# One expert slot fewer per layer, with the experts ordered by the row counts of three tiles

## The chip, the cores and the metric

The kernel runs on one core of one Trainium2 chip. The metric is the time of one execution in microseconds on the device. TensorE multiplies, VectorE, ScalarE and GpSimd do the element work, and the 16 DMA engines of the core move data. GpSimd issues the indexed transfers (gathers and scatters), ScalarE the stores and loads of whole row blocks, and SyncE the loads of weights.

## What is computed

The reference is one step of a two-layer decoder for a prompt group of 512 rows and a sample group of 64 rows, with the same weights for both and all arithmetic in float32. A layer has a mixer (spatial gating and differential attention) and then a mixture of 16 experts, which is where the change is:

```python
h = rmsnorm(x, g2).reshape(b * t, d)
pg = jax.nn.softmax((h @ r_g), axis=-1)          # 4 groups: the best one is taken
le_sel = ...                                     # the 4 experts of that group
tw, ti = lax.top_k(jax.nn.softmax(le_sel), 2)    # the best two of them
eidx = gi[:, None] * E_PER + ti
hg = jnp.einsum('nd,edf->nef', h, w_gate)
hu = jnp.einsum('nd,edf->nef', h, w_up)
a = jax.nn.silu(hg) * hu * gates[..., None]
return jnp.einsum('nef,efd->nd', a, w_down)
```

Each of the 576 rows goes to two experts of one group. An expert's weights are 1024 x 512 (gate and up) and 256 x 1024 (down).

## The kernel before

The 576 rows lie in five tiles of 128 (tile 4 holds the 64 sample rows). The order in which the tiles leave the mixer is `SEQ`: 0, 1, 2, 4, 3. For each tile TensorE multiplies by the output weights (`out_rows`, `sample_out`), VectorE adds (`add_out`), TensorE turns the tile (`turn_rows`) and computes router logits (`logit_parts`, `logit_sums`, `logits`), and VectorE marks the two experts of each row (`chosen`, result `M`). `token_ranks` sums `M` on TensorE, which gives every row its place among its expert's rows. ScalarE stores the normalised rows of each tile to `h_rows` (`store_rows`); the last store counts in `h_last`.

The experts are worked off in slots of 128 row places (`SLOTS`; an entry is a list of position, first row and width). A slot is one expert of up to 128 rows, or two or three parts of experts that share the 128 places. Positions are filled with experts by their row counts (`by_size` writes `order`); positions 0, 1 and 2 are fixed to the experts 0, 1 and 2 (`STILL`). There are 14 slots. Per slot: VectorE compares places with a row of numbers (`hot`, `main_group`), TensorE turns that into row indices (`index_rows`), VectorE writes them (`index`), GpSimd gathers the slot's rows (`gather_main`), TensorE turns them (`turn_in`), VectorE scales (`in_turned`), TensorE multiplies by gate and up in two halves (`up`), ScalarE and VectorE gate, TensorE turns (`turn_act`) and multiplies by down (`down`), ScalarE evacuates (`result`) and GpSimd scatters to `y_rows`. In a shared slot the parts are written as matmuls of 32 or 64 columns beside each other. The loop of TensorE runs `up` of slot n, `turn_act` of slot n-1, `up` second half, `index_rows` at slots 1, 3 and 5, `turn_in` of slot n+1, `down` of slot n-1.

The first slot is gathered earlier: `first_index` gives the rows of tiles 0, 1, 2 and 4, `gather_first` fetches them while the last tile is still in the mixer, `first_turn` turns them, and `first_late` adds the rows of the last tile.

SyncE loads the weights in pieces of 1 MB, three for each expert, in the order of first use (`LOADS`) into ten buffers. It waits at three places: for the end of the attention before the first piece, for `h_last` before the seventh, and for `order` before the first piece whose address depends on it. In the sample attention `sample_combine` writes the tile `fold`, which TensorE needs for `sample_turn`. `keep_busy` issues matmuls whose result nobody reads.

Of the kernel before, what the change touches and what calls it, by code (L numbers as in the profile page):

```python
# [19 lines left out]
P = 128  # L20
# [43 lines left out]
for _n, _w in _PAR:  # L64
# [5 lines left out]
NC32 = 8 * P + 64 + NT * 4 + 32 + E * E + 3 * E + 20  # L70
# [5 lines left out]
C_TIE, C_BASE, C_CAP = (slice(C_CLASS.stop + i * E, C_CLASS.stop + (i + 1) * E) for i in range(3))  # L76
C_PARTS = slice(NC32 - 20, NC32)
# [3 lines left out]
STILL = 3  # L81
CLASSES = [[0], [1], [2], [e for e in range(STILL, E) if e % EG != EG - 1], [e for e in range(E) if e % EG == EG - 1]]
FIRST_PLACE = [0, 1, 2, STILL, E - G]
SLOTS = [[(0, 0, 128)], [(1, 0, 128)], [(2, 0, 128)], [(3, 0, 128)], [(7, 0, 96), (3, P, 32)], [(4, 0, 128)], [(9, 0, 64), (10, 0, 64)], [(5, 0, 128)],
         [(6, 0, 128)], [(11, 0, 64), (15, 0, 64)], [(8, 0, 96), (12, P, 32)], [(12, 0, 128)], [(13, 0, 128)], [(14, 0, 128)]]
# [119 lines left out]
def program(nc, totals, d):  # L205
    Count.loops, Count.every, Count.layer = [], [], 0
    with ExitStack() as ctx:
# [70 lines left out]
        order_of = cat_cols[:, 256:512].rearrange("p (n e) -> p n e", n=E)  # L278
        moved = cat_cols[:, 3840:3840 + NT * (E - STILL) * E].rearrange("p (t n e) -> p t n e", t=NT, n=E - STILL)
# [108 lines left out]
        STEADY, EXTRA_BUFFERS = (6, 5, 7, 4, 8, 9, 2, 0, 3, 1), (2, 3, 6, 7, 8, 9)  # L388
        AHEAD = [4, 0, 5, 1, 2, 3]
# [53 lines left out]
        def _(sp):  # L443
# [8 lines left out]
            for l in layers():  # L452
                expert_at = {}
                for i in [*(AHEAD if l else range(RING)), *range(RING, W_LAYER)]:
# [24 lines left out]
                    if i >= N_DENSE:  # L479
                        pos, part = LOADS[i - N_DENSE]  # L480
                        if pos >= STILL:
                            if pos not in expert_at:
                                if not expert_at:
                                    sp.wait_ge(*dve_s.at("order"))
                                expert_at[pos] = sp.value_load(order[0:1, pos:pos + 1], min_val=0, max_val=E - 1)
                            at = expert_at[pos] * PER_EXPERT + (l * W_LAYER + N_DENSE + part)
                        else:
                            at = l * W_LAYER + N_DENSE + pos * PER_EXPERT + part
# [214 lines left out]
        def _(pe):  # L703
# [44 lines left out]
            for l in layers():  # L748
# [309 lines left out]

                def first_index():
# [36 lines left out]
                def after_sample(k):  # L1096
# [3 lines left out]
                    if k == HALF + 1:  # L1100
                        logit_sums(1)

                def after_last(n, k):
                    if (n, k) == (0, 2):
# [1182 lines left out]
```

## Time and profile before

| | us |
|---|---|
| median of 3 runs | 987.95 (983.75 to 988.01) |
| profiled execution | 987.82 |
| its span | 986.0 |
| PE busy | 946.2 (96%) |
| DVE busy | 397.1 (40%) |
| ACT busy | 249.4 (25%) |
| POOL busy | 191.9 (19%) |

PE is TensorE's matmul side, DVE VectorE, ACT ScalarE, POOL GpSimd, SPq SyncE's own queue. Times in a timeline are microseconds from the start of the span. The two layers repeat each other: what stands at time t in layer 0 stands about 485 us later in layer 1.

### The profile page before, as it was taken

How to read it: one execution, taken by the hardware profiler on the slowest of the kernel's cores; microseconds unless marked ns; L12 is line 12 of the kernel's file. 1: busy time of each engine (PE TensorE's matmuls, PEld its weight loads, DVE VectorE, ACT ScalarE, POOL GpSimd, SP SyncE). 2: the span in 40 equal slices, each digit the busy share in tenths (PEclk: the TensorE clock that was granted, in tenths of full speed). 3: DMA queues.
4: the chain of work that ended last, by engine and by line, in shares of the span. 5: the costliest groups of instructions: out<-in, count | busy, mean ns of one | idle time of the engine just before them, and what ended most of it. 6: DMA issues, size and time to landing. Idle time of an engine off the chain costs nothing.

```text
span 986.0 us, 12965 instructions
## 1 busy us (share of the span) xinstructions
PE 946.2 (96%) x4672; PEld 469.9 (48%) x4672; DVE 397.1 (40%) x991; ACT 249.4 (25%) x499; POOL 191.9 (19%) x267
## 2 busy tenths in 40 slices
PE   9999999999999999999899999999999999999991
PEld 6444445556445444434554344455564454444340
DVE  2403235676446562111343122556663575511114
ACT  2112346542011111111121123656221012111110
POOL 2333201331101111111124032023220012111100
PEclk9999999999999999999999999999999999999996
DMA  9716003341613979997842150225243169799946
GB/s 346 271 35 266 1 1 134 100 159 51 270 44 147 361 266 367 419 420 321 277 155 74 40 228 0 91 87 172 56 177 132 65 258 339 279 383 415 410 166 236
DMA packets 39769, 197.53 MB, mean 200 GB/s; under 512 B 7652, under 2 KB 7780, under 8 KB 23824
## 3 DMA queue, kind: packets, MB, share of 16 engines
q1 hardware_dynamic: 19456, 136.02, 35.2%
q0 software_dynamic: 15888, 45.80, 13.3%
q10 hardware_dynamic: 4352, 14.76, 4.2%
q8 instruction: 42, 0.69, 0.3%
q14 instruction: 31, 0.25, 0.1%
HBM read 177.24 MB, written 29.88 MB: 210 GB/s over the span
## 4 chain that ended last, share of the span: by engine, by line
PE 88%; DVE 5%; issue 2%; DMA 2%; ACT 1%; POOL 0%; POOLq 0%; DVEq 0%; ACTq 0%
PE ps L710 79%; PE ps L708 7%; PE ps L726 2%; DMA cat<-y_rows 1%; DVE cat L1933 1%; DMA hT<-h_rows,igat 1%; DVE hT L2075 0%; DMA y_rows<-hn,isca 0%; DVE hT L1555 0%; DVE tmp L1633 0%; DVE tmp L1688 0%; ACT L1386 0%; ACT L1340 0%; ACT L1374 0%; ACT ring L1374 0%
## 5 line engine op out<-in xcount | busy, mean ns | idle before, releaser
L710 PE MATMUL ps<-ring,hT 128*128 128x512 f32 (+3 forms) x1120 | 389.9, 582 | 1.2 <-ACT ring L1390 0.6
L710 PEld LDWEIGHTS ps<-ring,hT 128*128 128x128 f32 (+2 forms) x1120 | 153.0, 165 | 196.2 <-issue 192.7
L710 PE MATMUL ps<-ring,cat 128*128 128x512 f32 (+2 forms) x560 | 197.2, 598 | 0.0
L710 PEld LDWEIGHTS ps<-ring,cat 128*128 128x128 f32 (+2 forms) x560 | 72.4, 162 | 77.4 <-issue 75.7
L2075 DVE TENSOR_TENSOR hT<-ps,par 128x512 f32<-128x512 f32 x56 | 36.3, 686 | 170.1 <-PE ps L708 169.5
L651 POOL DMA_INDIRECT y_rows<-hn,isca x28 | 28.4, 1016 | 243.2 <-ACT hn L1466 228.5
L530 POOL TENSOR_TENSOR st<-st,half 128x1 f32<-128x1 f32 (+3 forms) x60 | 63.4, 1057 | 11.1 <-POOL st L528 10.9
L528 POOL TENSOR_SCALAR st<-st 128x1 f32<-128x1 f32 (+3 forms) x60 | 14.3, 239 | 243.4 <-DVE st L1576 83.3
L1576 DVE TENSOR_REDUCE st<-sqj 128x8 f32<-128x512 f32 x20 | 13.5, 681 | 111.5 <-ACT sqj L1302 111.4
L710 PE MATMUL ps<-hT,ring 128*128 128x512 f32 x128 | 57.1, 599 | 0.7 <-DVE tmp L1633 0.7
L1466 ACT COPY hn<-ps 128x1024 f32<-128x1024 f32 x26 | 26.3, 1012 | 102.2 <-PE ps L710 102.2
L536 POOL DMA_DIRECT2D kc<-in_ck x32 | 24.7, 772 | 94.7 <-PE ps L710 71.8
L1374 ACT ACTIVATE ring<-ps,st 128x128 f32<-128x128 f32 (+3 forms) x64 | 33.2, 524 | 27.6 <-DVE st L1700 27.5
L1302 ACT ACTIVATE sqj<-ps,st 128x512 f32<-128x512 f32 (+1 forms) x20 | 13.7, 686 | 96.9 <-PE ps L710 90.4
L710 PEld LDWEIGHTS ps<-hT,ring 128*128 128x128 f32 x128 | 23.7, 190 | 29.9 <-issue 28.4
L710 PE MATMUL ps<-vc,hT 128*128 128x512 f32 (+2 forms) x112 | 36.5, 598 | 0.9 <-issue 0.9
L643 POOL DMA_INDIRECT hT<-h_rows,igat x26 | 26.4, 1016 | 50.8 <-DVE isca L1973 44.7
L1449 ACT ACTIVATE cat<-ps 128x256 f32<-128x256 f32 x28 | 10.7, 383 | 97.4 <-PE ps L710 97.4
L536 POOL DMA_DIRECT2D vc<-in_cv x32 | 17.6, 550 | 88.4 <-PE ps L710 72.5
L1555 DVE TENSOR_TENSOR hT<-ps,g_sb 128x512 f32<-128x512 f32 x20 | 13.0, 686 | 53.3 <-PE ps L708 53.2
L1453 ACT COPY cat<-ps 128x256 f32<-128x256 f32 x28 | 10.4, 372 | 80.3 <-PE ps L708 80.3
L710 PE MATMUL ps<-kc,cat 128*128 128x512 f32 (+1 forms) x64 | 29.2, 594 | 0.0
(269 smaller groups left out, 1120.6 us busy)
## 6 DMA issues: line engine op xcount, KB each, us to landing
ring<-in_w SPq DMA_DIRECT2D x82, 1024.0 KB
kc<-in_w SPq DMA_DIRECT2D x12, 1024.0 KB
vc<-in_w SPq DMA_DIRECT2D x10, 1024.0 KB
v<-in_w SPq DMA_DIRECT2D x10, 1024.0 KB
kva<-in_w SPq DMA_DIRECT2D x10, 1024.0 KB
kc<-in_ck POOLq DMA_DIRECT2D x32, 256.0 KB, 3.5
vc<-in_cv POOLq DMA_DIRECT2D x32, 256.0 KB, 3.2
h_rows<-qk ACTq DMA_DIRECT2D x10, 512.0 KB, 2.6
```

The costliest lines, as they stand in the source:

```text
L528: nc.gpsimd.tensor_scalar(stat["ms"][at, 0:n], src, 1.0 / size, EPS, ALU.mult, ALU.add).then_inc(*pool_c.inc())
L530: nc.gpsimd.tensor_tensor(dst, stat["ms"][at, 0:n], half[at, 0:n], ALU.pow).then_inc(*pool_c.inc(*label))
L536: pool.dma_start(buffer(b % 2, g), view(d[table][bass.DynSlice(l * NPOOL + page, 1)])).then_inc(*arrived[b % 2].inc("kv", b, by=16))
L643: pool.indirect_dma_start(hs[:, b, :], None, h_rows, bass.IndirectOffsetOnAxis(index, 0), bounds_check=TOK - 1, oob_is_err=False).then_inc ...
L651: pool.indirect_dma_start(rows, bass.IndirectOffsetOnAxis(index, 0), y_sb[:, b, :], None, bounds_check=rows.shape[0] - 1, oob_is_err=False ...
L708: ins = pe.transpose(out, lhsT, rhs)
L710: ins = pe.matmul(out, lhsT, rhs, start=start, stop=stop, skip_group_check=loose)
L726: pe.matmul(bank(u)[0:cols, 0:cols], operand, operand)
L1302: nc.scalar.activation(sqj[at, t % 2, :], bank(u)[at, :], ACT.Square, scale=stat["rs"][at, t:t + 1]).then_inc(*act_s.inc("sq", name, t))
L1374: ins = nc.scalar.activation(e_sb[:, n % 2, m, 0:(i + 1) * P], bank(f"S{n % 2}", m)[:, 0:(i + 1) * P], ACT.Exp, bias=stat["nb"][:, c:c + 1 ...
L1466: nc.scalar.copy(y_sb[:, b, :], ps[:, 6:8, :].rearrange("p a n -> p (a n)")).then_inc(*read["O"].inc("down", *key))
L2075: vec.tensor_tensor(hsT[:, b, hf * HALF:(hf + 1) * HALF, :], bank(f"T{hf}").rearrange("p (j t) -> p j t", j=HALF), g, ALU.mult).then_inc(* ...
```

## The change

- `order` is now written from the row counts of the tiles 0, 1 and 2 alone (`part_counts` on TensorE, then `by_size`), before the last two tiles are routed. To that end the logits of tile 2 are computed earlier, inside `sample_out`. No position is fixed; position 3 has the largest count of its class.
- 13 slots in place of 14. Seven of them are shared (four before).
- Each of the 16 positions is looked up, so SyncE's first piece waits for `order`. The wait for `h_last` still stands before the seventh piece.
- The places of the first three positions are computed by the new `places_ahead`, once before `first_hot` for four tiles and once for the last tile; those of the other 13 (`places_by_size`) ahead of the slot loop instead of in slot 1. `lower_of` is cut in two.
- `index_rows(1)` stands in the middle of the first `up` half instead of before it.
- `sample_combine` stands ahead of the mixing and scaling work of its step (`FOLD_AT`).
- The buffers of the first ten pieces and the order of the next layer's first six pieces (`STEADY`, `AHEAD`) follow the new order of use.

```diff
-STILL = 3
-CLASSES = [[0], [1], [2], [e for e in range(STILL, E) if e % EG != EG - 1], [e for e in range(E) if e % EG == EG - 1]]
-SLOTS = [[(0, 0, 128)], [(1, 0, 128)], [(2, 0, 128)], [(3, 0, 128)], [(7, 0, 96), (3, P, 32)], [(4, 0, 128)], [(9, 0, 64), (10, 0, 64)], [(5, 0, 128)],
-         [(6, 0, 128)], [(11, 0, 64), (15, 0, 64)], [(8, 0, 96), (12, P, 32)], [(12, 0, 128)], [(13, 0, 128)], [(14, 0, 128)]]
+AHEAD_POS = 3
+CLASSES = [[e for e in range(E) if e % EG != EG - 1], [e for e in range(E) if e % EG == EG - 1]]
+RANK_OF = [3, 2, 1, 0, *range(4, E)]
+SLOTS = [[(0, 0, 128)], [(1, 0, 128)], [(2, 0, 128)], [(4, 0, 96), (2, P, 32)], [(9, 0, 64), (10, 0, 64)], [(3, 0, 128)], [(5, 0, 96), (3, P, 32)],
+         [(6, 0, 96), (8, 0, 32)], [(7, 0, 96), (8, 32, 32)], [(11, 0, 64), (15, 0, 64)], [(13, 0, 128)], [(14, 0, 96), (12, P, 32)], [(12, 0, 128)]]
...
-                        if pos >= STILL:
-                            if pos not in expert_at:
-                                if not expert_at:
-                                    sp.wait_ge(*dve_s.at("order"))
+                        if pos not in expert_at:
+                            if not expert_at:
+                                sp.wait_ge(*dve_s.at("order"))
...
+                def part_counts():
+                    claim("I")
+                    for t in SEQ[:3]:
+                        pe.wait_ge(*dve_s.at("M", t))
+                        mm(bank("I")[:, 6 * E:7 * E], c16[:, B_ONES], M[:, t * E:(t + 1) * E], start=(t == SEQ[0]), stop=(t == SEQ[2]),
+                           inc=full["I"].inc("counted") if t == SEQ[2] else None)
...
+                    if k == HALF + 2:
+                        logit_parts(2)
...
-                        logit_parts(2)
+                        part_counts()
...
-                index_rows(1)
+                def second_index(j):
+                    if j == 1:
+                        index_rows(1)
...
+                    if n in FOLD_AT:
+                        sample_combine(FOLD_AT[n])
                     for name, j in SMALL.get(n, []):
...
+                def places_ahead(tiles):
+                    n, cols = tiles.stop - tiles.start, slice(tiles.start * E, tiles.stop * E)
+                    link(vec.scalar_tensor_tensor(tmp[:, 400:400 + NT * E][:, cols], selB[:, cols], 1024.0, R[:, cols], ALU.mult, ALU.add))
+                    link(vec.tensor_tensor(moved_ahead[:, tiles], marked[:, tiles].unsqueeze(2).to_broadcast([P, n, AHEAD_POS, E]),
+                                           order_of[:, 0:AHEAD_POS, :].unsqueeze(1).to_broadcast([P, n, AHEAD_POS, E]), ALU.mult))
+                    link(vec.tensor_reduce(both_ahead[:, tiles], moved_ahead[:, tiles], AX.X, ALU.add))
+                    low = rows_of[:, tiles, 0:AHEAD_POS, 3]
+                    link(vec.tensor_scalar(low, both_ahead[:, tiles], 1000.0, None, ALU.is_gt))
+                    link(vec.scalar_tensor_tensor(placed_by[:, tiles, 0:AHEAD_POS], low, -1024.0, both_ahead[:, tiles], ALU.mult, ALU.add))
...
                 lower_of(2)
+                by_size()
...
                 in_turned(0, ("m", 0), (0,))
+                lower_of(TP - 1)
+                places_ahead(slice(TP - 1, TP))
                 hot(1, slice(TP - 1, TP), 1)
...
-                by_size()
                 hot(0, slice(TP - 1, TP), 0)
                 index(2)
+                places_by_size()
```

Three places of the program show where instructions move. The first is SyncE's queue from the end of the attention on (`kc`, `vc`, `v`, `kva` and `ring` are the piece buffers, in brackets stand the semaphores waited for). Before:

```order
L489 DMA kc<-in_w 128x2048 [waits k_stored,full_T1,v_stored,full_O,piece_used]
L489 DMA ring<-in_w 128x2048 [waits piece_used]
L489 DMA vc<-in_w 128x2048 [waits piece_used]
L489 DMA ring<-in_w 128x2048 [waits piece_used]
L489 DMA v<-in_w 128x2048 [waits piece_used]
L489 DMA kva<-in_w 128x2048 [waits piece_used]
L489 DMA ring<-in_w 128x2048 [waits h_last,piece_used]
```

And with the change, down to the third piece:

```order
L489 TENSOR_LOAD order [waits k_stored,v_stored,full_T1,dve_s,full_O,piece_used]
L489 ISA x2
L491 ISA
L491 DMA kc<-in_w 128x2048
L491 ISA [waits piece_used]
L491 DMA ring<-in_w 128x2048
L489 TENSOR_LOAD order [waits piece_used]
L489 ISA x2
L491 ISA
L491 DMA vc<-in_w 128x2048
```

The look-up of `order`, with its wait for VectorE (`dve_s`), now stands ahead of the first piece.

The second is VectorE between the routing of tile 4 and the indices of the first gather (`ifirst`). Before:

```order
L1869 SCALAR_TENSOR_TENSOR o_sb<-ps,M 128x48
L1869 SCALAR_TENSOR_TENSOR o_sb<-ps,M 128x16
L1879 TENSOR_TENSOR cat<-o_sb,c 128x384
L1879 TENSOR_TENSOR cat<-o_sb,c 128x128
L1555 TENSOR_TENSOR hT<-ps,par 128x4x128
L1916 TENSOR_REDUCE o_sb<-ps 128x1
L1918 TENSOR_SCALAR ifirst<-o_sb 128x1
```

And with the change:

```order
L1903 SCALAR_TENSOR_TENSOR o_sb<-ps,M 128x48
L1903 SCALAR_TENSOR_TENSOR o_sb<-ps,M 128x16
L1892 SCALAR_TENSOR_TENSOR tmp<-o_sb 128x80
L1893 TENSOR_TENSOR tmp<-tmp,oS 128x240
L1895 TENSOR_REDUCE tmp<-tmp 128x15
L1897 TENSOR_SCALAR rows_of<-tmp 128x5x3
L1898 SCALAR_TENSOR_TENSOR o_sb<-rows_of,tmp 128x5x3
L1912 TENSOR_TENSOR cat<-o_sb,c 128x384
L1912 TENSOR_TENSOR cat<-o_sb,c 128x128
L1574 TENSOR_TENSOR hT<-ps,par 128x4x128
L1974 TENSOR_REDUCE o_sb<-ps 128x1
L1976 TENSOR_SCALAR ifirst<-o_sb 128x1
```

The five instructions of `places_ahead` stand ahead of the two that write the first slot's comparison.

The third is TensorE from the late rows of the first slot (`oS,qk`) into its first `up` half (`kc,hT`); `rows_of` are the index matmuls. Before:

```order
L710 MATMUL ps<-oS,qk 128x128 x8
L710 MATMUL ps<-rows_of,cat 128x4 x5
L710 MATMUL ps<-kc,hT 128x512 x4
L710 MATMUL ps<-rows_of,cat 128x4 x5
L710 MATMUL ps<-ring,hT 128x512 x4
```

And with the change:

```order
L712 MATMUL ps<-oS,qk 128x128 x8
L712 MATMUL ps<-kc,hT 128x512 x2
L712 MATMUL ps<-rows_of,cat 128x4 x5
L712 MATMUL ps<-kc,hT 128x512 x2
L712 MATMUL ps<-rows_of,cat 128x4 x5
```

The index matmuls of slot 1 moved behind two matmuls of slot 0.

## Rows read from the trace of the kernel before

**Rows 1.** The page: span, and the chain that ended last.

```profile
span 986.0 us, 12965 instructions
...
PE 88%; DVE 5%; issue 2%; DMA 2%; ACT 1%; POOL 0%; POOLq 0%; DVEq 0%; ACTq 0%
```

**Rows 2.** Timeline of PE in the slots: start, duration, line, operands, count, [idle before].

```profile
331.68 3.60 PE L710 MATMUL ps<-v,cat 128*128 128x512 f32 x8
...
343.08 3.60 PE L710 MATMUL ps<-ring,cat 128*128 128x512 f32 x8
...
358.86 3.64 PE L710 MATMUL ps<-ring,hT 128*32 128x512 f32 x32
362.43 0.44 PE L708 MATMUL ps<-c,cat 128*128 128x128 f32 x2
...
479.43 0.27 PE L708 MATMUL ps<-c 128*128 128x128 f32 x1
```

**Rows 3.** SyncE's queue: timeline of its issues, and its longest wait (total, times, longest).

```profile
244.54 0.33 SPq L489 DMA_DIRECT2D kc<-in_w  x1
...
311.78 8.49 SPq L489 DMA_DIRECT2D ring<-in_w  x4
...
SPq L477 <- DMA h_rows<-qk: 128.4, 2, 64.2
```

**Rows 4.** Windows: engines' busy time, granted clock, DMA share, GB/s.

```profile
262.00:311.70 49.70, 48.55 (x258) 25.50 (x257) 25.11 (x98) 7.26 (x13) 4.39 (x9) 1.00 0.15 58
363.00:455.00 92.00, 92.00 (x448) 38.04 (x441) 17.08 (x38) 14.09 (x24) 14.42 (x15) 1.00 0.99 399
```

**Rows 5.** Timeline of DVE from the sample rows' sum to the order.

```profile
285.75 1.38 DVE L1771 TENSOR_TENSOR x<-x,ps 64x512 f32<-64x512 f32 x2
...
292.94 0.18 DVE L1833 COPY lg<-ps 128x20 f32<-128x20 f32 x1 [3.49 <-PE ps L710]
...
295.60 0.74 DVE L1549 TENSOR_SCALAR qk<-x,st 128x1024 f32<-128x1024 f32 x1
...
300.66 0.76 DVE L1879 TENSOR_TENSOR cat<-o_sb,c 128x384 bf16<-128x384 f32 x2
...
314.98 0.16 DVE L1939 SCALAR_TENSOR_TENSOR st<-st,c 128x16 f32<-128x16 f32 x1
315.18 0.42 DVE L1941 TENSOR_TENSOR cat<-st 128x256 f32<-128x256 f32 x1
...
318.13 0.17 DVE L1948 CAST order<-st 128x16 int32<-128x16 f32 x1
```

**Rows 6.** Timeline of PE around the first two slots.

```profile
301.48 0.25 PE L710 MATMUL ps<-rows_of,cat 128*128 128x4 bf16 x4
...
307.58 2.03 PE L710 MATMUL ps<-c,ws 128*128 128x128 f32 x16
...
320.31 1.07 PE L708 MATMUL ps<-c,hT 128*128 128x128 f32 x8
...
329.87 0.96 PE L710 MATMUL ps<-rows_of,cat 128*128 128x4 bf16 x40 [0.70 <-DVE cat L1933]
```

**Rows 7.** POOL: first two gathers, then scatters' landing at 340 to 460, at 960 to 986.

```profile
303.32 1.17 POOL L627 DMA_INDIRECT ws<-h_rows,ifirst  x1 [13.80 <-issue]
...
314.74 1.09 POOL L643 DMA_INDIRECT hT<-h_rows,igat  x1 [6.86 <-DVE isca L1973]
...
DMA to landing us min/median/max: 4.5/8.6/9.7
...
DMA to landing us min/median/max: 4.0/4.1/4.2
```

**Rows 8.** The wait for `fold` in the attention: timelines of PE and DVE, windows around.

```profile
236.95 0.88 PE L710 MATMUL ps<-fold,ring 128*128 128x64 f32 x6 [1.03 <-DVE fold L1759]
...
234.46 0.68 DVE L1688 TENSOR_TENSOR tmp<-ps,par 128x512 f32<-128x512 f32 x1
...
236.59 0.31 DVE L1759 TENSOR_SCALAR fold<-c,st 128x64 f32<-128x64 bf16 x1
...
238.50:241.80 3.30, 3.30 (x34) 2.89 (x36) 1.77 (x2) 0.00 (x0) 0.00 (x0) 0.50 0.00 0
484.60:487.60 3.00, 3.00 (x14) 3.00 (x15) 0.00 (x0) 0.00 (x0) 0.00 (x0) 0.50 0.65 223
```

More of the change, by code:

```diff
@@ L1167, in turn_in, with up @@
                     pending.append((hs_used[b], ("tr", *key)))
-                def up(b, key, hf, parts):
+                def up(b, key, hf, parts, between=None):
                     u = f"S{b}"
@@ L1180, in up @@
                                inc=full[u].inc("gu", *key) if (k == KD - 1 and at.stop == P) else None)
+                        if between:
+                            between(j)
                 def turn_act(b, key):
@@ L1221, in _ @@
                     if n < NSLOT:
-                        up(b, ("m", n), 0, weights(n, 0))
+                        up(b, ("m", n), 0, weights(n, 0), None if n else second_index)
                         free(len(FREED[n, 0]))
@@ L1427, in _ @@
                 for m, t in enumerate(SEQ):
+                    if t == TP:
+                        logit_parts(2)
                     if t == SEQ[-1]:
@@ L1851, in chosen, with higher_of @@
                     dve.wait_ge(*dve_s.at("M", t))
-                def lower_of(t):
+                def higher_of(t):
                     mine = slice(t * E, (t + 1) * E)
@@ L1873, in _, with by_size @@
                 iota = c32[:, C_IOTA]
-                place = R.rearrange("p (t e) -> p t e", t=NT)
                 def hot(s, tiles, label=None):
                     n = tiles.stop - tiles.start
-                    ins = vec.tensor_tensor(onehot[:, s % 4, tiles, :], place[:, tiles, s].unsqueeze(2).to_broadcast([P, n, P]), across(iota[:, 0:P], n, P), ALU.is_equal)
+                    ins = vec.tensor_tensor(onehot[:, s % 4, tiles, :], placed_by[:, tiles, s].unsqueeze(2).to_broadcast([P, n, P]), across(iota[:, 0:P], n, P), ALU.is_equal)
                     if label is not None:
                         ins.then_inc(*dve_s.inc(*(("first_hot",) if label == "first" else ("onehot", label))))
+                def by_size():
+                    size, at = stat["size"], stat["at"]
+                    names = c32[:, C_SLOTS][:, 16:16 + E]
+                    dve.wait_ge(*full["I"].at("counted"))
+                    vec.scalar_tensor_tensor(size, bank("I")[:, 6 * E:7 * E], float(E), c32[:, C_TIE], ALU.mult, ALU.add).then_inc(*read["I"].inc("counted"))
+                    dve.wait_ge(*read["I"].at("counted"))
+                    pairs = cat_cols[:, 0:E * E].rearrange("p (a b) -> p a b", a=E)
+                    link(vec.tensor_tensor(pairs, across(size, E, E), wide(size, E, E), ALU.is_gt))
+                    link(vec.tensor_tensor(pairs, pairs, groups(c32[:, C_CLASS], E, E), ALU.mult))
+                    link(vec.tensor_reduce(at, pairs, AX.X, ALU.add))
+                    link(vec.tensor_tensor(at, at, c32[:, C_BASE], ALU.add))
+                    link(vec.tensor_tensor(order_of, across(at, E, E), wide(c32[:, C_RANK], E, E), ALU.is_equal))
+                    link(vec.tensor_tensor(pairs, order_of, across(names, E, E), ALU.mult))
+                    link(vec.tensor_reduce(size, pairs, AX.X, ALU.add))
+                    vec.tensor_copy(order[:, :], size).then_inc(*dve_s.inc("order"))
                 add_out(0, 1)
@@ L1889, in _ @@
                 chosen(0)
+                higher_of(0)
                 lower_of(0)
+                for flat_of in (selB, R):
+                    vec.memset(flat_of[:, (TP - 1) * E:TP * E], 0.0)
                 add_out(0, 2)
@@ L1897, in _ @@
                 chosen(1)
+                higher_of(1)
                 lower_of(1)
                 add_sample_out()
+                chosen(2)
                 turned(TP)
-                chosen(2)
+                higher_of(2)
                 lower_of(2)
+                by_size()
                 scaled(TP)
@@ L1905, in _ @@
                 chosen(TP)
+                higher_of(TP)
                 lower_of(TP)
@@ L1908, in _ @@
                 places((slice(0, (TP - 1) * E), slice(TP * E, NT * E)), NT - 2)
+                places_ahead(slice(0, NT))
                 def early_hot(m, label=None):
@@ L2102, in _ @@
                         index(0)
-                        places_by_size()
                     if n == 2:
```

74 lines of the change are left out of this document (33 added, 41 removed).

## The prediction, made before the changed kernel ran

> **What bounds the kernel now.** I read the page first. Its chain of waits is 88% PE in a span of 986.0 us [rows 1]: TensorE sets the time, and a wait elsewhere counts only where TensorE stands still. So I went through TensorE's timeline in the expert stage. The `down` matmuls of slots 0 and 1 begin at 331.68 and 343.08, so a full slot takes 11.40 us; the first half of a shared slot takes 3.64 us against 3.60 for a full half's eight matmuls, with a turn of 0.44 us behind it; the stage ends at 479.43 [rows 2]. Next came SyncE's queue, since the change touches its order: the first six pieces go out from 244.54, then it waits 64.2 us for the last row store, and sends four more from 311.78 [rows 3]. The windows show what lies in that gap: from 262 to 311.7 the DMA engines are 0.15 busy, and from 363 to 455 they are 0.99 busy at 399 GB/s [rows 4]. One piece of 1 MB then takes 1.049/0.399 = 2.63 us. The reader is to keep two things: the gap is quiet, and it is where the first two gathers run.
>
> **The change part by part, for one layer.**
>
> *Slots.* One full slot goes: -11.4 us [rows 2]. Three more are shared. A shared slot has the same columns in each half plus dearer turns (0.44 where the turn at 479.43 takes 0.27) and something at each half's edges, 0.04 by the row and doubled here for the second part. Three halves at 0.08 and two turns at 0.17 make 0.58 us, so 3 x 0.58 = +1.75. Below it could be 3 x 0.22 = 0.7, above 3 x 1.0 = 3.
>
> *Indices.* The groups of index matmuls grow from 40, 40 and 15 to 55, 55 and 25, 40 more. Forty take 0.96 us: +0.96. The 0.70 us wait for VectorE ahead of one of them should go, as `places_by_size` moves ahead of the loop: -0.7 [rows 6]. That work, some 3 us, now lies beside the first `up` of slot 0 and the wait for the second gather, which cover it; uncovered it would delay `in_turned` of slot 1 by those 3 us.
>
> *Fold.* TensorE waits 1.03 us for `fold`, which is done at 236.90. The operation of 0.68 us and its followers, which stand ahead of it from 234.46, move behind it, so it comes up to 2 us earlier and the wait goes. What is late in its place is only scaling work on VectorE, which is busy 40% of the time. Behind the wait the granted clock is 0.50 for 3.30 us though PE is busy throughout [rows 8]. That is the level of 1.2 GHz after a short idle stretch. At the full clock those 3.3 us would be 1.65 at best. VectorE is busy for 2.89 of them, so I take 1.2 of the 1.65 as a loss that ends with its cause. Fold: -1.03 - 1.2 = -2.2, with bounds of -1.0 and -2.7.
>
> Without the front of the stage that makes -11.4 + 1.75 + 0.96 - 0.7 - 2.2 = -11.6 us per layer.
>
> *The first six pieces.* Before, they are in their buffers by about 262. Now they wait for `order`. VectorE has the sample rows' sum at 285.75 + 1.38 = 287.1. Then come `chosen(2)` and `lower_of(2)`, 295.60 - 292.94 = 2.7 us; the copies of `turned(TP)`, 1.3 us (between one and two times the 0.74 of a 128x1024 operation); and `by_size`, from 314.98 to 318.30, 3.3 us [rows 5]. `order` is ready near 294.4. I give SyncE one us for the look-up (its group of four issues around `order` runs to 320.27, 2 us behind it, which is the upper bound [rows 3, 5]), so the first piece goes near 295.4, and six of 2.63 us keep the DMA engines full to about 311.2, landing by 313. The pieces themselves are in time or almost, since their first use stands behind the turn of the first gather at 307.58 [rows 6] and that of the late rows. What counts is what they collide with.
>
> *First gather.* Its issue stood at 303.32, and TensorE's turn of its rows began at 307.58 [rows 6, 7], 4.3 us later. `places_ahead` puts five dependent operations ahead of the comparison (0.76 us) on which it rests: two with up to 240 columns, near the 0.42 of a 128x256 one, and three at 0.16: +1.3 us [rows 5]. TensorE reached `first_index` at 301.48 without a wait [rows 6], so nothing swallows this. Issue: 304.6, in the middle of the six pieces. How long it takes to land among them no row shows for this place. The bounds are indexed transfers on a quiet queue, 4.1 us, and those amid weights from 340 to 460, 8.6 us at the median and 9.7 at most [rows 7]. With pieces queued up to 311.2 this place is nearest to the loaded stretch, and I take 8.6: 4.3 later than before. `first_turn` starts 1.3 + 4.3 = 5.6 us late. The last row store crosses the same load; that delays only the seventh piece.
>
> *Second gather.* Its issue stood at 314.74 [rows 7] and rests on the late rows of slot 0, which follow `first_turn`. It moves by 5.6, by 0.2 for the two more operations in the chain of the late rows, and by 1.65 for `lower_of` and `places_ahead` of the last tile (two and five operations at the durations above) which now stand ahead of its comparison: 322.2. It used to be in use after 5.6 us (320.31), with four pieces just sent. Now it runs with ten in succession; between 5.6 and 8.6 I take 8.0, nearer to the loaded row. TensorE turns slot 1 at 330.2, so 9.9 us later than before, and in the two waits it has nothing real to do for about 5 and 4 us. What is queued behind them is the whole slot loop. So the front costs +9.9.
>
> *Clock.* At the layer's end the clock stands at 0.50 for 3.0 us with PE busy [rows 8]. After two waits as long, the same may follow each: at most 2 x 1.7 = 3.4, at least nothing. `keep_busy` matmuls fill part of them; I take 0.8. The Trainium skill ("TensorE: Matmul & The Clock Gate") says that an idle array is set back to 1.2 GHz; whether these waits are enough no row here shows.
>
> *Sum.* -11.6 + 9.9 + 0.8 = -0.9 us per layer, -1.8 for two. From the profiled 987.82 that gives 986.0; this execution lies 0.1 below the median of 987.95, so the same figure stands for a median.
>
> **Rivals.**
>
> *The queues take turns fairly.* If a gather's packets alternate with those of a piece and are not held behind the backlog, a gather of 0.5 MB (1.3 us at 399 GB/s) pays about its own length again: 1.3 us for each. Then the front costs 1.3 + 0.2 + 1.65 for the issues and about 1.9 for both transfers, 5.0, and the clock 0.4: -6.2 per layer, 975.4. For it: the least landing amid weights was 4.5 us. Against: the median there was 8.6 [rows 7]. The Trainium skill ("DMA: Bandwidth & Descriptors", on queues, rings and completion order) says each DMA engine goes round its queues packet by packet, which is this rival; the median of 8.6 against 4.1 speaks for a longer delay than that rule alone suggests. Chance 0.20, 971 to 980.
>
> *No collision at all.* If the six pieces are through, or `order` is ready so early that they are, only the 3.15 us of later issue stay: -8.4 per layer, 971.0. It needs the first piece by 288, and VectorE's sum of the sample rows stands at 287.1 [rows 5]; or a gather that load does not slow. Chance 0.07.
>
> *The weights run out (slower).* Before, the last expert is first used in the last slot, some 12 us before 479.43, thus near 467, while the DMA engines are saturated only to 455 [rows 2, 4]. Now 13 slots need the same 48 pieces, and positions 14 and 12 both come in slot 11, the last but one, near 456. The transfers save one gather and one scatter (2.6 us) and start the seventh piece about 1.6 us later, ending near 454 to 457. The margin shrinks from 12 to about 1.5 us. It decides once the pieces of position 12 land behind the start of slot 11; each piece short costs 2.63 us, and one to two of them make +3 per layer: 987.8 + 2 x (-0.9 + 3) = 992.0. For it: the 0.99. Against: the main case shifts the slots late anyway, which gives the transfers time. Chance 0.15, 988 to 996.
>
> *It doesn't do what it says.* Counts of three tiles may put an expert with more rows than its places at a narrow position, and extra slots then run: +11.4 each, 997 and up; or both waits pay the whole clock price and a loaded gather takes 9.7. Chance 0.05.
>
> **How the numbers follow.** The main case has 0.53. Its own range is 979 (shorter landings by 2 us, full fold gain) to 991 (clock and shared slots at their upper bounds). A measurement of this kernel tells about 0.5% from no change, here 983.0 and 992.9. Of the main case 0.16 lies below, 0.32 within and 0.05 above; the fair queues and the absent collision give 0.27 below; the weights 0.06 within and 0.09 above, the last 0.05 above. Faster 0.43, same 0.38, slower 0.19. The whole range cuts the lower part of the absent collision and of the fair queues, and the upper end of the last two cases: 972 to 993.
>
> **What would show it.** Right: SyncE's first expert piece near 295 and its sixth landing near 313; a wait of about 5 us before the turn of the first gathered rows, and of about 4 before the turn of slot 1; a granted clock of 0.5 behind them; at 238 to 242 no wait for `fold` and a clock of 1.0; 13 slots of 11.4 to 12 us; an end of the first expert stage near 478.5. Wrong: gathers that land in 5 us or less (fair queues); no DMA traffic around 304 (no collision); TensorE waiting for pieces in slots 9 to 11 (weights); a fourteenth slot. The prediction fails on its smallest margin: -11.6 and +10.7 nearly cancel, and the landing time of two gathers decides the sign.

## The result, and the profile of the changed kernel

The changed kernel takes 994.28 us (median of 11 executions, 991.05 to 998.94) against 985.22 (11 executions, 983.65 to 988.01): 0.9% longer, ratio 1.0087 with an interval of 1.0071 to 1.0104. The forecast was 986.0 and a range of 972 to 993.

The two profiled executions tell less than the medians do. That of before took 987.82, 2.6 above its median, and that of the changed kernel 991.05, 3.2 below its own. Between them lie 3.2 us, between the medians 9.1. So what follows takes the mechanisms from the traces and the sizes from medians.

The page of the changed kernel shows the span, two DMA queues (packets, MB, share; q1 has the weights, q0 the gathers and scatters) and the chain that ended last:

```profile
span 989.3 us, 13927 instructions
...
q1 hardware_dynamic: 19456, 136.03, 35.0%
q0 software_dynamic: 15312, 45.72, 13.3%
...
PE 85%; DMA 6%; DVE 4%; issue 2%; ACT 1%; DVEq 0%; ACTq 0%; POOLq 0%; POOL 0%
```

DMA has grown from 2% of the chain [rows 1] to 6%, and PE fell from 88% to 85%. The timeline of PE shows where TensorE waits for transfers (start, duration, what, idle time before and what ended it); first layer 0, then layer 1:

```profile
234.25 0.78 PE L712 MATMUL ps<-fold,ring 128*128 128x64 f32 x6
...
298.54 0.25 PE L712 MATMUL ps<-rows_of,cat 128*128 128x4 bf16 x4 [1.54 <-DVE cat L1912]
...
309.13 3.78 PE L712 MATMUL ps<-c,ws 128*128 128x128 f32 x16 [1.67 <-DMA ws<-h_rows,ifirst]
...
328.82 1.97 PE L710 MATMUL ps<-c,hT 128*128 128x128 f32 x8 [4.57 <-DMA hT<-h_rows,igat]
330.83 5.28 PE L712 MATMUL ps<-vc,hT 128*128 128x512 f32 x8
...
341.52 3.60 PE L712 MATMUL ps<-ring,cat 128*128 128x512 f32 x8
...
480.13 0.27 PE L710 MATMUL ps<-c 128*128 128x128 f32 x1
...
785.63 0.25 PE L712 MATMUL ps<-rows_of,cat 128*128 128x4 bf16 x4 [1.54 <-DVE cat L1912]
...
796.67 3.78 PE L712 MATMUL ps<-c,ws 128*128 128x128 f32 x16 [4.78 <-DMA ws<-h_rows,ifirst]
...
816.06 1.97 PE L710 MATMUL ps<-c,hT 128*128 128x128 f32 x8 [4.27 <-DMA hT<-h_rows,igat]
```

The wait for `fold` [rows 8] is gone; one of 0.43 us for `tmp` just ahead of it has grown to 0.86. From the `down` of slot 0 to the end of the slots it is 480.13 - 341.52 = 138.6 us, where it was 479.43 - 331.68 = 147.7 [rows 2]: the slot is saved. But that first `down` stands at 341.52 and stood at 331.68. TensorE waits for the first indices, for the first gathered rows and for those of slot 1, and behind each wait it is slow: the first turn takes 3.78 us (2.03 in [rows 6]), the turn of slot 1 takes 1.97 (1.07), its `up` half 5.28.

The timeline of SyncE's queue shows what the gathers ran into, the first and the last of the pieces in question:

```profile
291.44 0.36 SPq L491 DMA_DIRECT2D kc<-in_w  x1
...
313.44 2.95 SPq L491 DMA_DIRECT2D ring<-in_w  x4
```

The same of POOL, the first two gathers:

```profile
300.38 1.17 POOL L629 DMA_INDIRECT ws<-h_rows,ifirst  x1 [15.24 <-issue]
...
319.94 1.09 POOL L645 DMA_INDIRECT hT<-h_rows,igat  x1 [13.53 <-DVE isca L2018]
```

And the windows (busy time of PE, PEld, DVE, ACT and POOL, granted clock, DMA share, GB/s):

```profile
238.50:241.80 3.30, 3.30 (x29) 2.27 (x26) 2.48 (x5) 1.25 (x3) 0.00 (x0) 1.00 0.02 5
301.00:306.00 5.00, 5.00 (x17) 3.52 (x17) 1.87 (x4) 1.15 (x2) 1.21 (x3) 0.50 1.02 428
...
324.00:329.00 5.00, 0.43 (x7) 0.34 (x6) 0.36 (x2) 0.38 (x1) 0.00 (x0) 0.82 1.01 418
329.00:336.00 7.00, 6.95 (x17) 3.66 (x17) 5.39 (x14) 0.00 (x0) 0.00 (x0) 0.64 0.50 204
...
786.00:791.00 5.00, 4.32 (x26) 2.98 (x25) 2.00 (x6) 1.15 (x2) 1.31 (x2) 1.00 1.03 431
```

The first gather goes out at 300.38 into DMA engines that are full (1.02 at 428 GB/s), and its rows are turned at 309.13, 8.7 us later; before it was 4.3. The second needs 8.9 us (319.94 to 328.82), before 5.6. From 301 to 306 TensorE is busy all the time at a granted clock of 0.50, the level of 1.2 GHz, after a wait of 1.54 us; at 238.5, where the wait for `fold` is gone, it is 1.00. In layer 1 the same wait of 1.54 us is followed by a clock of 1.00 (786 to 791), and TensorE then waits 4.78 us for the rows where it waited 1.67 in layer 0. So the half clock ahead of the first turn costs nothing by itself, as the rows are late either way. What costs is the half clock on the work behind the long waits.

### The profile page after: what moved, and what is told of

The parts are those of the page before. It is cut to its first block, busy times and chain, and to the rows that moved or that the text cites. A ratio compares the mean times of both kernels' runs of the same rounds, so it can differ in the third digit from the quotient of the medians.

```text
span 989.3 us, 13927 instructions
## 1 busy us (share of the span) xinstructions
PE 936.4 (95%) x5122; PEld 454.6 (46%) x5122; DVE 397.2 (40%) x1007; ACT 245.8 (25%) x493; POOL 190.4 (19%) x263
## 3 DMA queue, kind: packets, MB, share of 16 engines
q1 hardware_dynamic: 19456, 136.03, 35.0%
q0 software_dynamic: 15312, 45.72, 13.3%
## 4 chain that ended last, share of the span: by engine, by line
PE 85%; DMA 6%; DVE 4%; issue 2%; ACT 1%; DVEq 0%; ACTq 0%; POOLq 0%; POOL 0%
PE ps L712 77%; PE ps L710 7%; DMA ws<-h_rows,ifirst 2%; DMA hT<-h_rows,igat 2%; DMA qk<-y_rows 1%; DMA cat<-y_rows 1%; PE ps L728 1%; DMA y_rows<-hn,isca 0%; DVE x L2126 0%; DVE hT L1574 0%; DVE tmp L1652 0%; DVE tmp L1707 0%; DVE hT L2120 0%; ACT L1403 0%; ACT L1357 0%
## 5 line engine op out<-in xcount | busy, mean ns | idle before, releaser
L712 PE MATMUL ps<-ring,hT 128*128 128x512 f32 (+3 forms) x1312 | 397.1, 584 | 0.9 <-ACT ring L1407 0.6
L712 PEld LDWEIGHTS ps<-ring,hT 128*128 128x128 f32 (+2 forms) x1312 | 150.5, 152 | 197.2 <-issue 193.6
L712 PE MATMUL ps<-ring,cat 128*128 128x512 f32 (+2 forms) x560 | 184.0, 600 | 0.0
L712 PEld LDWEIGHTS ps<-ring,cat 128*128 128x128 f32 (+2 forms) x560 | 65.4, 157 | 78.2 <-issue 76.5
L2120 DVE TENSOR_TENSOR hT<-ps,par 128x512 f32<-128x512 f32 x52 | 33.9, 687 | 160.4 <-PE ps L710 157.7
L1485 ACT COPY hn<-ps 128x1024 f32<-128x1024 f32 x24 | 24.3, 1012 | 94.5 <-PE ps L712 94.5
L712 PE MATMUL ps<-kva,hT 128*32 128x512 f32 (+1 forms) x128 | 43.7, 596 | 0.0
L710 PE MATMUL ps<-c,hT 128*128 128x128 f32 x192 | 27.7, 290 | 8.8 <-DMA hT<-h_rows,igat 8.8
L710 PEld LDWEIGHTS ps<-c,hT 128*128 128x128 f32 x192 | 22.4, 148 | 21.1 <-issue 12.1
```

Source lines behind the costliest of these rows:

```text
L710: ins = pe.transpose(out, lhsT, rhs)
L712: ins = pe.matmul(out, lhsT, rhs, start=start, stop=stop, skip_group_check=loose)
L1485: nc.scalar.copy(y_sb[:, b, :], ps[:, 6:8, :].rearrange("p a n -> p (a n)")).then_inc(*read["O"].inc("down", *key))
L2120: vec.tensor_tensor(hsT[:, b, hf * HALF:(hf + 1) * HALF, :], bank(f"T{hf}").rearrange("p (j t) -> p j t", j=HALF), g, ALU.mult).then_inc(* ...
```

## The experiments

All times below are medians of 4 to 10 executions, with the ratio to the kernel before as run beside them on the same chip (its own median lay between 985.1 and 985.9).

**early_pieces** takes the collision out of the first gather.

```diff
-                        if pos not in expert_at:
+                        if pos < 2:
+                            at = l * W_LAYER + N_DENSE + pos * PER_EXPERT + part
+                        elif pos not in expert_at:
```

> The changed kernel, except that the six pieces of the first two positions are loaded from the fixed experts 0 and 1 at once and SyncE waits for `order` only ahead of the third position; the output is therefore not the reference's. If the collision of the six pieces with the two gathers is what costs, the first gather lands about 4.3 us after its issue instead of 8.5, TensorE keeps its full clock at the turn of the gathered rows, and only the later issues stay (1.5 + 0.2 + 1.65 us a layer of the 14.3 that the front lost): 994.3 - 2 x 10.9 = 972.5, between 970 and 977. If the longer chain of VectorE operations ahead of the gathers is what costs, the time stays above 988.

981.97 us (978.21 to 986.13), ratio 0.9963 (0.9941 to 0.9985): 12.3 us less than the changed kernel, where 21.8 were expected. (Of the six pieces five go out at once, from 240.28 to 242.45. The sixth is the first of the third position, which is still looked up, and goes at 291.55, long before the gather.) The timeline of PE says why it is less:

```profile
306.06 2.03 PE L715 MATMUL ps<-c,ws 128*128 128x128 f32 x16
...
324.55 1.97 PE L713 MATMUL ps<-c,hT 128*128 128x128 f32 x8 [5.35 <-DMA hT<-h_rows,igat]
```

The first gather is cured: no wait and 2.03 us for the turn. The second is not. The timeline of POOL has its issue, 9.6 us ahead of its use, and that of SyncE's queue the four pieces sent before it:

```profile
314.90 1.09 POOL L648 DMA_INDIRECT hT<-h_rows,igat  x1 [8.54 <-DVE isca L2021]
```

```profile
310.39 2.50 SPq L494 DMA_DIRECT2D ring<-in_w  x4
```

Neither theory had this. Here four pieces go out within 2.5 us of 310.39. In the kernel before, the group of four took 8.49 us [rows 3], and a row of its waits (total, times, longest) that had gone unused names the reason:

```profile
SPq L484 <- DVE order L1948: 11.2, 2, 5.7
```

The wait for `order` held the ninth piece for 5.7 us, and in that gap the second gather landed. An `order` that is known early takes this gap away as well.

**late_pieces** puts the collision into the kernel before, with one line ahead of SyncE's first piece:

```diff
                     if i == N_DENSE + FIRST_OTHER:
+                        sp.wait_ge(*dve_s.at("M", 2))
```

> The kernel before with one line more: SyncE holds its first piece until VectorE has marked tile 2 (near 294). Nothing else changes. If the collision costs, it shows alone: the first gather, issued at 303.3, lands after 8.5 us instead of 4.3, the second one after 8 to 9 instead of 5.6, and the clock falls behind both waits: +8 to +10 us a layer, 1001 to 1005. If the chain of VectorE is what costs, 985 to 989.

1004.51 us (1003.59 to 1005.76), ratio 1.0186 (1.0169 to 1.0203): +19.3, as much as the collision theory had, but by one gather and not by two. In its timeline of PE all of it comes from the first gather; the second, which has its gap, is in time:

```profile
313.59 3.78 PE L711 MATMUL ps<-c,ws 128*128 128x128 f32 x16 [7.65 <-DMA ws<-h_rows,ifirst]
...
328.29 1.07 PE L709 MATMUL ps<-c,hT 128*128 128x128 f32 x8
```

The timeline of POOL has the first gather's issue:

```profile
304.55 1.17 POOL L628 DMA_INDIRECT ws<-h_rows,ifirst  x1 [16.82 <-issue]
```

It is 9.0 us ahead of its use (4.3 before). It is also late itself: 4.9 us behind the index matmuls (1.8 in [rows 6, 7]), as it waits for a row store that needs 8.8 us to land among the pieces; before, such a store needs 2.6 to 2.8. Pieces that come late are by themselves enough to make the old kernel slower than the changed one.

**before_fold** is the kernel before with the early fold alone (the two lines of the diff that move `sample_combine`).

> The kernel before with `sample_combine` alone moved ahead of the mixing and scaling work. By the changed kernel's trace the wait of 1.03 us and the half clock behind it go, 2.6 to 2.8 us a layer: 985.2 - 5.4 = 979.8. If only the wait goes and the clock falls anyway: 983. If the time is given back at a later wait of the attention: 985.

981.36 us (980.55 to 983.21), ratio 0.9965 (0.9953 to 0.9977): -3.9, thus 1.9 a layer. It lies between the two values, and they aren't told apart by the median. The granted clock from 238.5 to 241.8 is 1.00 in its trace, 0.50 before, so the clock part is there; part of the wait comes back in front of it, where TensorE waits 0.85 us for `tmp` (0.43 before).

**quiet13** has 13 slots and the front of the kernel before:

```diff
-CLASSES = [[0], [1], [2], [e for e in range(STILL, E) if e % EG != EG - 1], ...]
-SLOTS = [[(0, 0, 128)], [(1, 0, 128)], [(2, 0, 128)], [(3, 0, 128)], [(7, 0, 96), (3, P, 32)], ...
+FIXED = [5, 9, 13]
+CLASSES = [[5], [9], [13], [e for e in range(E) if e % EG != EG - 1 and e not in FIXED], ...]
+SLOTS = [[(0, 0, 128)], [(1, 0, 128)], [(2, 0, 128)], [(3, 0, 128)], [(5, 0, 96), (3, P, 32)], [(4, 0, 128)], [(8, 0, 64), (9, 0, 64)],
+         [(6, 0, 96), (10, 0, 32)], [(7, 0, 96), (10, 32, 32)], [(11, 0, 64), (15, 0, 64)], [(13, 0, 128)], [(14, 0, 96), (12, P, 32)], [(12, 0, 128)]]
```

> 13 slots without the new front: the kernel before with the early fold, with three fixed positions as before (but experts 5, 9 and 13, whose rows let the other counts fit), `order` from all rows, pieces at the old time, and the slot table cut to 13 slots. If the slots are worth what the changed kernel's trace shows between the first and the last `down` (9.1 us a layer) and nothing of its front is needed for it: 985.2 - 5.4 - 18.3 = 961.5. If the transfers can't keep up with 13 slots that start 10 us earlier, TensorE waits for pieces in the last slots: 966 to 976.

970.57 us (966.58 to 972.83), ratio 0.9836 (0.9806 to 0.9865). 9 us short of the first theory and within the second's. PE's timeline has waits for pieces and, at the layer's end, for rows:

```profile
443.74 3.64 PE L711 MATMUL ps<-ring,hT 128*32 128x512 f32 x32 [1.22 <-DMA ring<-in_w]
...
483.57 1.97 PE L709 MATMUL ps<-c,x 128*128 128x128 f32 x8 [2.90 <-DVE x L2151]
```

And a window:

```profile
350.00:360.00 10.00, 10.00 (x71) 3.91 (x72) 8.29 (x30) 1.39 (x2) 2.02 (x2) 1.00 0.46 156
```

Ninety us before the first of these waits the DMA engines were half idle: SyncE's queue, which waits for a free buffer, sent nothing between 344.2 and 356.24.

**early_ninth** gives the second gather its gap back, on top of early_pieces:

```diff
+                    if i == N_DENSE + BUFFERS - RING + 4:
+                        sp.wait_ge(*hs_in[1].at("hs", "m", 1))
```

> As early_pieces (changed kernel, first two positions' pieces from the fixed experts 0 and 1, so the output is not the reference's), and SyncE also holds the ninth piece until the second gather has landed. In the kernel before, the wait for `order` held that piece until 319.4, after which the gather was in; with `order` known early nothing holds it, and in early_pieces the second gather took 9.6 us to land against 5.6. If the pieces behind the eighth are what delays it, it lands in about 5.5, its wait of 5.2 us shrinks to 1 or 2, the clock stays up: -4.1 - 2.5 us a layer, 982.0 - 13 = 969. If the later issue of the gather is what costs, it stays at 980 to 984. If the held pieces then come short in the last slots: 973 to 978.

969.48 us (965.65 to 972.23), ratio 0.9844 (0.9821 to 0.9868). Another 12.5 us, as the collision theory gave it. In PE's timeline the wait of 5.35 us is one of 0.41, and the turn is at full clock:

```profile
318.28 1.09 PE L715 MATMUL ps<-c,hT 128*128 128x128 f32 x8 [0.41 <-DMA hT<-h_rows,igat]
319.83 3.67 PE L717 MATMUL ps<-vc,hT 128*128 128x512 f32 x8 [0.46 <-issue]
```

The wait of 1.53 us for the first indices is still in this trace, but here the clock doesn't fall behind it:

```profile
301.00:306.00 5.00, 4.31 (x32) 3.60 (x31) 3.18 (x10) 2.29 (x3) 1.42 (x3) 1.00 0.28 75
```

**paced** is the changed kernel with holds alone: SyncE waits for the first gather ahead of the third piece and for the second ahead of the seventh.

```diff
+                    if i == N_DENSE + BUFFERS - RING + 2:
+                        sp.wait_ge(*hs_in[1].at("hs", "m", 1))
+                    if i == N_DENSE + 2:
+                        sp.wait_ge(*hs_in[0].at("hs", "m", 0))
```

> The changed kernel with the collisions taken out and nothing else: SyncE sends two pieces after `order`, waits for the first gather to land, sends four, waits for the second gather, sends the rest. If the two collisions are the loss: both gathers land in 4.3 to 6 us, TensorE waits 1.5 us for the first indices and 1 to 2 for slot 1, the clock stays up. That alone would give about 970; the transfers start some 10 us later than in quiet13 with two pieces fewer in the buffers, so waits for pieces in slots 9 to 11 of 2 to 4 us a layer come on top: 972 to 978, 975. If the loss is in VectorE's longer chains: above 985.

976.51 us (972.25 to 984.5), ratio 0.9910 (0.9884 to 0.9937): two waits of SyncE turn the changed kernel from 0.9% slower into 0.9% faster. 17.8 of the 24.8 us that the two collisions cost come back. The rest is the second gather. It goes out at 316.80 (313.56 in early_ninth), TensorE waits 2.52 us for it, and the first `down` stands at 332.20 (328.92). That gather needs the last row store, which takes 8.3 us to land among the four pieces sent behind the first gather, and 2.6 in early_ninth, which sends none there. The expected waits for weights in the slots 9 to 11 didn't come: in the slots no wait for a piece reaches 0.4 us. So 975 was nearly met, but by another sum.

**busy** tests the clock. It fills the three waits with matmuls that nobody reads (`keep_busy(6)`, `keep_busy(18)` and `keep_busy(17)`).

> The changed kernel with matmuls that nobody reads in its three waits: 6 ahead of the first indices, 18 ahead of the turn of the first gathered rows, 17 ahead of the turn of slot 1. Gathers are as late as before. If the half clock behind the waits costs what the trace shows (1.8 us in the first turn, 0.9 and 1.6 in the turn and `up` of slot 1, 0.5 between), the granted clock stays 1.0 there and the time falls by 4.8 us a layer: 984.7. If the clock loss is hidden in the waits themselves or the matmuls only take the place of waiting: 992 or more.

988.59 us (986.39 to 992.26), ratio 1.0042 (1.0025 to 1.0058): -5.7, between the two values. In the timeline of PE the gathers are as late as in the changed kernel, but the turns are short:

```profile
308.98 2.05 PE L712 MATMUL ps<-c,ws 128*128 128x128 f32 x16 [0.22 <-DMA ws<-h_rows,ifirst]
...
328.61 3.67 PE L712 MATMUL ps<-vc,hT 128*128 128x512 f32 x8 [0.46 <-issue]
...
454.57 0.63 PE L712 MATMUL ps<-v,hT 128*32 128x512 f32 x3 [0.93 <-SPq L167]
...
491.73 1.32 PE L710 MATMUL ps<-c,x 128*128 128x128 f32 x8 [1.36 <-DVE x L2200]
```

The window from 301 to 306, at a clock of 0.50 in the changed kernel:

```profile
301.00:306.00 5.00, 4.32 (x34) 3.74 (x33) 3.22 (x10) 2.30 (x3) 1.39 (x3) 1.00 1.01 424
```

First turn, turn and `up` of slot 1 are 1.7 + 0.9 + 1.6 = 4.2 us shorter. A part is lost again later in the layer, where TensorE now waits 0.93 us ahead of a matmul on the piece buffer `v` and 1.36 for rows (0.47 in the changed kernel).

**quiet13_four** tried to give quiet13 more weights ahead: expert 1 fixed as a fourth position, five shared slots, and the wait for `h_last` replaced by one for the first gather.

> quiet13 with its supply of weights moved ahead: a fourth position fixed (expert 1), so that the seventh to tenth piece need no `order`, and these wait for the landing of the first gather in place of the last row store; the slot table has five shared slots. quiet13 waited 1.2 to 3 us a layer for pieces in the slots 10 and 11. If that was the supply, two pieces (5.3 us) more in the buffers by the second gather end it: 970.6 - 5 = 965.5. If the four pieces now collide with the last row store and the second gather, its landing goes from 5.6 to 8 or 9 us and TensorE waits 3 us in slot 1 at a falling clock: 972 to 976.

978.66 us (977.93 to 982.93), ratio 0.9926 (0.9909 to 0.9942): a miss, slower by 8 us than quiet13 in the way that its rival said, and beyond that rival's 972 to 976. Three things change at once here, so the run doesn't tell what more weights ahead are worth by themselves. The second gather goes out at 314.65 (310.25 in quiet13) and TensorE waits 4.91 us for it, with the turn at half clock again:

```profile
321.08 1.97 PE L709 MATMUL ps<-c,hT 128*128 128x128 f32 x8 [4.91 <-DMA hT<-h_rows,igat]
```

**known_first** goes on from early_ninth and moves `places_ahead` behind the first comparison, whose expert is a constant.

> As early_ninth (first two positions' pieces from the fixed experts 0 and 1, so the output is not the reference's), and the first slot's comparison takes the places of an expert written in as a constant (8 in layer 0, 13 in layer 1, the ones that `order` puts there), so that the five operations of `places_ahead` stand behind it and not ahead. If the longer chain costs TensorE what the trace shows (1.5 us of waiting for the first indices, some 1.3 of half clock behind it), 969.5 - 5.6 = 963.9. If the weights already bound the last slots, what is gained in front is waited for there: 968 to 970.

963.71 us (961.38 to 964.93), ratio 0.9775 (0.9756 to 0.9794): -5.8, where the chain theory had -5.6. These are medians of four executions each, and the two traces don't show that much: the wait of 1.53 us is gone, but the first `down` stands at 328.17 against 328.92. The trace of early_ninth is that of its fastest execution (965.65) and has no half clock behind this wait. That its other executions had one would explain the difference of the medians; no trace shows it.

**quiet13_light** loads half of each of the last twelve pieces of a layer:

```diff
+                    cols = 2 * W if i >= W_LAYER - 12 else 4 * W
```

> quiet13 with only half of each of the last twelve weight pieces of a layer loaded (the output is therefore not the reference's; TensorE's work is the same). If the transfers bound quiet13, its waits of 1.2 us in layer 0 and 1.4 and 1.6 us in layer 1 for pieces in slots 10 and 11 go, and with them most of the 2.9 us of waiting for the rows at the layer's end: 970.6 - 6 = 964.6. If not, it stays at 969 to 972.

958.61 us (957.60 to 959.70), ratio 0.9730 (0.9713 to 0.9747). Transfers cost quiet13 twelve us, twice the expected six.

**paced33** is paced with three pieces ahead of the first gather and three behind, and six matmuls that nobody reads ahead of the first indices.

> paced with three pieces ahead of the first gather's landing and three behind it (paced: two and four), and six matmuls that nobody reads ahead of the first indices. The last row store and the second gather meet less traffic, so the wait of 2.5 us for slot 1 shrinks to about 0.5, and the clock stays at full behind the first indices: 976.5 - 2 x (2.0 + 1.3) = 970. If the weights bound the last slots by then: 973 to 976.

976.73 us (974.50 to 979.79), ratio 0.9919 (0.9891 to 0.9946): no different from paced, and a miss. The second gather went out at 317.37, no earlier, and the wait for slot 1 was longer (3.91 us in layer 0). That gather waits for the last row store, and the trace shows it delayed by the pieces: 10.1 us to land (8.3 in paced, 2.6 in early_ninth). The matmuls ahead of the first indices did their part (a wait of 0.20 us, a clock of 1.00 from 301 to 306), but what they gained was waited for in slot 1.

**quiet13_even** orders the slots of quiet13 so that pieces are used up sooner:

```diff
-         [(3, 0, 128)], [(5, 0, 96), (3, P, 32)], [(4, 0, 128)], [(8, 0, 64), (9, 0, 64)], [(6, 0, 96), (10, 0, 32)], [(7, 0, 96), (10, 32, 32)],
+         [(5, 0, 96), (3, P, 32)], [(8, 0, 64), (9, 0, 64)], [(3, 0, 128)], [(6, 0, 96), (10, 0, 32)], [(7, 0, 96), (10, 32, 32)], [(4, 0, 128)],
```

> quiet13 with the same slots in another order: the two slots that bring two new experts each (positions 5 and 3, 8 and 9) stand in places 3 and 4, before the full slots of the positions 3 and 4. In quiet13 all ten buffers were full from 343.9 to 356.2 and the transfers stood at a share of 0.46 from 350 to 360, some 5 us of transfer that its last slots and its layer's end then waited for (1.2 us and 2.9 in layer 0). If transfers bound quiet13 (quiet13_light says 12 us of it), pieces used up sooner let the next ones start sooner: 970.6 - 2 x 3.5 = 963.6, between 961 and 967. If the buffers are full anyway, only later: 969 to 972.

963.74 us (961.35 to 965.35), ratio 0.9774 (0.9752 to 0.9797), as expected and 2.3% faster than the kernel before. The same window has twice the traffic:

```profile
350.00:360.00 10.00, 10.00 (x82) 4.60 (x76) 7.99 (x29) 1.77 (x3) 2.02 (x2) 1.00 0.91 366
```

In the timeline of PE no slot waits 0.4 us or more for a piece, and the wait at the layer's end is shorter:

```profile
479.45 1.32 PE L709 MATMUL ps<-c,x 128*128 128x128 f32 x8 [2.29 <-DVE x L2151]
```

The three fixed experts are a choice that suits the row counts of this input (5, 9 and 13 have 124, 116 and 48 rows in layer 0); with other counts an extra slot may run, as it may in the kernel before.

## Why the prediction was wrong

In us per layer, predicted and measured (differences of medians halved, except for the slots, which are from the trace):

| term | predicted | measured | by |
|---|---|---|---|
| slots and indices | -9.4 | -9.1 | 147.7 and 138.6 in the two traces |
| fold | -2.2 | -1.9 | before_fold |
| chain ahead of the first indices | +1.3 | +2.9 | known_first against early_ninth |
| first gather among the six pieces | +4.3 | +6.2 | early_pieces against the changed kernel |
| second gather | +4.3 | +6.2 | early_ninth against early_pieces |
| clock | +0.8 | in the three above | |
| sum | -0.9 | +4.3 | |

Twice 4.3 is 8.6; the medians differ by 9.1, so the terms close to 0.2 a layer. The slots and the fold are within 0.3 each of what was predicted. The front is not: 10.7 with the clock, and 15.3 measured.

The failing step is **"I take 0.8" for the clock**. The landings themselves were sized nearly right: 8.6 and 8.0 predicted, 8.7 and 8.9 read in layer 0. What stood behind them was not. The prediction counted two waits that could cost the clock and chose a value near zero because `keep_busy` fills part of them. Both cost it in full: behind the first gathered rows the turn takes 3.78 us where busy has 2.05, and behind the wait for slot 1 the turn and the `up` half take 1.97 and 5.28 where busy has 1.09 and 3.67. That makes 4.2 us a layer in the rows, more than the upper bound of 3.4 that the prediction named; busy, which leaves the gathers late, gives 2.9 on the median. The Trainium skill ("TensorE: Matmul & The Clock Gate") has an idle array fall back to 1.2 GHz; the granted clock of 0.50 behind the long waits, and 1.00 in busy, agree.

In the traces this step closes the account. Three marks of PE, the `hn` matmuls of either layer and the last turn, before:

```profile
41.59 1.16 PE L710 MATMUL ps<-hn 128*128 128x128 f32 x8 [0.62 <-DVE hn L1582]
...
526.48 1.16 PE L710 MATMUL ps<-hn 128*128 128x128 f32 x8 [0.62 <-DVE hn L1582]
...
964.70 0.27 PE L708 MATMUL ps<-c 128*128 128x128 f32 x1
```

And with the change:

```profile
39.97 1.16 PE L712 MATMUL ps<-hn 128*128 128x128 f32 x8 [0.62 <-DVE hn L1601]
...
527.06 1.16 PE L712 MATMUL ps<-hn 128*128 128x128 f32 x8 [0.62 <-DVE hn L1601]
...
967.80 0.27 PE L710 MATMUL ps<-c 128*128 128x128 f32 x1
```

From the first mark to the second it is 484.9 us and 487.1, from the second to the third 438.2 and 440.7: +2.2 and +2.5. The forecast of -0.9 with 4.2 in place of 0.8 is +2.5. The medians are further apart, 4.5 a layer. The changed kernel's trace is of the fastest of its eleven executions; what the other 2 us a layer are in the middle ones no trace shows, and they stay open. The first mark also says that the trace of before was 1.6 us late from its start on. That and the gain of the fold, which the prediction didn't carry into its times, are why the first piece went out at 291.44 and the first gather at 300.38, each about 4 us ahead of the forecast.

The extra 1.6 us of the chain ahead of the first indices are a difference of medians alone: the wait is 1.54 us in both layers, near the 1.3 of the prediction. The clock behind it was 0.50 in one layer and 1.00 in the other.

The second gather was right in size in part by luck. "Ten in succession" was meant as a longer queue; the prediction didn't see that the wait for `order`, 5.7 us on the ninth piece, was what had kept the way clear before. An edit that made `order` early took a wait away from SyncE, and that wait had done work. On the other side the later issue of this gather (+1.85 in the working) was counted in full and costs little by itself: with the way clear, as in early_ninth, TensorE waits 0.41 us for it. The two errors offset each other.

*Fair queues* was priced too low, and its rule is not shown to have failed. It was given 1.3 us for the first gather. The page of the profile says that a weight packet has 136.03 MB / 19456 = 7.0 KB and one of the gathers and scatters 45.72 / 15312 = 3.0 KB, both as means. Packet for packet a gather of 0.52 MB would get 3 parts in 10 of 418 GB/s. As an estimate that is 4.2 us for the gather instead of 1.3, so 4.3 + 2.9 = 7.2 us of landing, 1.5 below the measured 8.7. The Trainium skill ("DMA: Bandwidth & Descriptors", queues, rings and completion order) states turns by the packet; that its packets are those of the profile is assumed here. Taken so, the rule gives most of the landing time of the loaded rows [rows 7], not the 5.6 us (4.3 + 1.3) that the rival drew from it. The remaining 1.5 us stay open, and no run tells turns by the packet from a gather that is held behind the backlog.

*The weights run out* did not come in the changed kernel, as its late front gave the transfers time. It came in quiet13, whose front is some 10 us earlier, for 12 us by quiet13_light. The reason that the prediction gave (more new experts in the last slots) is only part of it: at 350, when transfers could have run, SyncE had no free buffer.

The base was a small error of its own: the sum started from an execution 2.6 us above what turned out to be the median of eleven. Against that median the forecast of -1.8 us would have been 983.4.

## What to carry to other kernels

A wait on a queue that has nothing to do with the engine which ends the kernel may be what keeps the way clear for one that has: before an edit makes something known earlier, read which transfers that wait was holding, and hold them by a wait of their own (two such waits took the changed kernel from 994.3 to 976.5 us). Price a stall of TensorE of 4 to 5 us with the half clock on the work behind it (4.2 us a layer here); behind a wait of 1.5 us the clock fell in some traces and not in others. When buffers are full early and short late, try the order in which the work uses them up: the same slots in another order gave 7 us.

## What the runs showed of the hardware

- A gather beside large transfers is slowed far beyond its own length: 4.3 us to its use on a quiet way, 8.7 to 9.6 among 1 MB pieces (changed kernel, early_pieces), while the DMA engines as a whole still moved 418 to 428 GB/s. A row store of 0.5 MB takes 2.6 us on a quiet way, 8.3 to 10.1 among pieces (late_pieces, paced, paced33).
- A wait of 1.54 us is followed by 5 us at a granted clock of 0.50 in layer 0 of the changed kernel (301 to 306), by 1.00 in its layer 1 (786 to 791) and by 1.00 in early_ninth; with matmuls that nobody reads in it the clock stays at 1.00. Why the same wait does one or the other was not tried.
- The changed kernel's executions spread over 7.9 us, those of the kernel before over 4.4. Why it spreads more was not tried.
